# Retention stage: the first gate product among the state products, the gate products one tile ahead, the turns of finished tiles behind the outputs

## The reference, cut to what matters

```
inner = einsum('bnihd,bnjhd->bnhij', qc, kc) * dmat        # per tile of 128 tokens, 4 heads
o_inner = einsum('bnhij,bnjhe->bnihe', inner, vc)
kv = einsum('bnjhd,bnjhe->nbhde', k_dec, vc)               # per tile, forward and backward
s_end, s_start = scan(lambda s, kv_n: (chunk_decay * s + kv_n, s), s0, kv)
o_cross = einsum('bnihd,nbhde->bnihe', q_dec, s_start)
ret = head_group_norm(o_fwd + o_bwd, ret_gn) * silu(gr)    # gr: columns of the input projection
```

## Time and profile before

| | us |
|---|---|
| time, median of 3 runs (2480.75 to 2486.7) | 2484.94 |
| the profiled execution's own time | 2485.23 |
| its span, first to last instruction | 2483.4 |
| PE busy in the span (88%) | 2189.6 |
| DVE busy (48%) | 1194.3 |
| ACT busy (33%) | 811.9 |
| POOL busy (10%) | 241.3 |

### The profile page before, as it was taken

One profiled execution on the slowest core, in us unless ns is written; L12 is line 12 of the kernel. 1 busy time (PEld: TensorE's weight loads), 2 busy tenths in 40 slices (PEclk: granted clock), 3 DMA queues, 4 the chain that ended last, 5 costly groups with the idle time before them and its releaser, 6 DMA issues.

```text
span 2483.4 us, 25328 instructions
## 1 busy us (share of the span) xinstructions
PE 2189.6 (88%) x10527; PEld 1654.5 (67%) x10527; DVE 1194.3 (48%) x1490; ACT 811.9 (33%) x998; POOL 241.3 (10%) x200
## 2 busy tenths in 40 slices
PE   1999989899999969999759999997999996799992
PEld 0587765388886547777637766645888844677771
DVE  0293234232322468887556622524223235788883
ACT  1123423010000137777432244211000012577771
POOL 2132010100000020000021301002000000100002
PEclk9999989999999969999979998998999996899996
DMA  7225330211124369999641334011021133799983
GB/s 267 88 88 203 136 145 1 102 52 68 35 102 153 110 233 373 381 381 377 244 168 68 131 122 158 9 68 51 35 102 68 54 125 119 277 378 386 381 338 144
DMA packets 113877, 417.13 MB, mean 168 GB/s; under 512 B 7768, under 2 KB 9928, under 8 KB 89056
## 3 DMA queue, kind: packets, MB, share of 16 engines
q1 hardware_dynamic: 89056, 329.27, 35.7%
q0 software_dynamic: 19920, 68.31, 7.4%
q10 hardware_dynamic: 4784, 17.87, 1.8%
HBM read 378.89 MB, written 36.54 MB: 167 GB/s over the span
## 4 chain that ended last, share of the span: by engine, by line
PE 71%; DVE 16%; ACT 6%; issue 3%; DMA 3%; SPq 0%; ACTq 0%; PEldq 0%; POOL 0%; DVEq 0%; POOLq 0%
PE ps L645 60%; DVE expert_low L1827 7%; ACT expert_high L1364 2%; PE ps L760 2%; PE ps L656 2%; PE ps L773 2%; DVE x_low L1833 2%; DMA ring_lo<-in_w_mod_dram 1%; ACT branch L1397 1%; ACT x_high L1369 1%; DVE work L1852 1%; DVE hidden_low L1839 1%; DVE work L1595 1%; PE ps L911 1%; PE ps L761 1%
## 5 line engine op out<-in xcount | busy, mean ns | idle before, releaser
L1827 DVE TENSOR_TENSOR expert_low<-ring_lo,expert_high 128x2048 fp32r<-128x2048 f32 x192 | 432.9, 2285 | 26.9 <-ACT expert_high L1364 26.9
L1364 ACT ACTIVATE expert_high<-ring_lo 128x2048 fp32r<-128x2048 f32 x192 | 367.3, 1915 | 158.7 <-PE ps L645 133.1
L645 PE MATMUL ps<-ring_lo,hT 128*128 128x512 f32 (+1 forms) x800 | 314.5, 552 | 12.5 <-ACT hT L1198 12.3
L645 PEld LDWEIGHTS ps<-ring_lo,hT 128*128 128x128 f32 x800 | 150.9, 191 | 164.1 <-issue 160.4
L645 PE MATMUL ps<-expert_high,x_high 128*128 128x512 f32 x512 | 207.5, 405 | 9.6 <-DVE expert_low L1827 9.6
L645 PE MATMUL ps<-branch,ring_lo 128*128 128x320 f32 x768 | 214.4, 432 | 0.0
L645 PE MATMUL ps<-expert_high,x_low 128*128 128x512 f32 x512 | 201.9, 394 | 0.0
L645 PE MATMUL ps<-expert_low,x_high 128*128 128x512 f32 x512 | 200.9, 392 | 0.0
L1313 ACT ACTIVATE work<-ps 128x640 f32<-128x640 f32 x48 | 33.7, 703 | 501.7 <-PE ps L645 501.7
L645 PE MATMUL ps<-h_hi,w_hi 128*128 128x320 f32 x768 | 186.2, 324 | 1.7 <-issue 1.7
L645 PEld LDWEIGHTS ps<-branch,ring_lo 128*128 128x128 f32 x768 | 143.6, 190 | 53.3
(11 more groups left out here) (272 smaller groups left out, 3195.6 us busy)
## 6 DMA issues: line engine op xcount, KB each, us to landing
ring_lo<-in_w_gate_dram SPq DMA_DIRECT2D x64, 1024.0 KB, 8.4
ring_lo<-in_w_up_dram SPq DMA_DIRECT2D x64, 1024.0 KB, 7.1
ring_lo<-in_w_down_dram SPq DMA_DIRECT2D x64, 1024.0 KB, 7.5
ring_lo<-in_w_in_dram SPq DMA_DIRECT2D x26, 2048.0 KB, 7.9
ring_lo<-in_w_mod_dram SPq DMA_DIRECT2D x24, 2048.0 KB, 13.0
y_dram<-branch ACTq DMA_DIRECT2D x32, 512.0 KB, 8.9
ring_lo<-in_w_out_dram SPq DMA_DIRECT2D x4, 2048.0 KB, 8.9
work<-mod_dram POOLq DMA_DIRECT2D x12, 512.0 KB, 9.0
```

Of the source, the lines that this page charges most:

```text
L645: return pe.matmul(out, lhsT, rhs, start=(k == 0), stop=(k == n - 1))
L1364: A(e_high[n % HIGH], e_raw[n % RAW], ACT.Copy).then_inc(ec_a.sem, 1)
L1827: TT(out=e_low[n % RAW], in0=e_raw[n % RAW], in1=e_high[n % HIGH].bitcast(F32), op=ALU.subtract).then_inc(el_v.sem, 1)
```

## The change

PE makes state products 0 and 1, then the gate product of tile 0, then state products 2 to 7, then turns q and k of tile 0. In the loop it makes the gate product of the next tile, the inner product of this one, the turns of q and k of the next, the outputs of this one, and last the turn of the finished result of the tile before. Outputs now also wait until the tile before has been normed (bank 6), which the turn of that tile did earlier. Silu's result has five buffers, one for each tile, in a part of `branch` that held the zeros and the modulation rows; ACT therefore waits for the transfers out of them before the first Silu. ACT takes Silu and k one tile ahead. DVE copies q of the next tile after the outputs of this one are there, before it norms them, and waits for the turn of the tile before ahead of overwriting `o_tmp`.

```diff
--- before.py
+++ after.py
@@ -548,7 +548,7 @@
         sf_st = [w_(11776 + 512 * n, 512) for n in range(NS)]
         rqT, rqTf, rqTb, rkT = (w_(13824 + 512 * n, 512).rearrange("p (h i) -> p h i", h=HR) for n in range(4))
         inner = [w_(15872 + 512 * b, 512).rearrange("p (h i) -> p h i", h=HR) for b in range(2)]
-        sgr = w_(16896, 512)
+        sgr = [branch[:, 8 * T + 512 * t:8 * T + 512 * (t + 1)] for t in range(NT)]
         gu = w_(8192, NT * 512).rearrange("p (t c) -> p t c", t=NT)
         gv = w_(10752, NT * 512).rearrange("p (t c) -> p t c", t=NT)
         cmb = [w_(13824 + 512 * b, 512) for b in range(2)]
@@ -821,7 +821,9 @@
 
 
                 w(pe, e_a, l, NU)
-                for n, (_, tt) in enumerate(STATES):
+                def state_product(n):
+
+                    tt = STATES[n][1]
                     w(pe, kd_g, l, n + 1)
                     if n >= 2:
                         w(pe, kv_v, l, n - 1)
@@ -830,32 +832,23 @@
                         i = pe.matmul(ps[:, n % 2, hs], kdec[n % 2][:, hs], zr[:, tt, 2, hs], start=True, stop=True)
                     i.then_inc(kv_p.sem, 1)
 
-                def turn_ret(tt):
-                    w(pe, rn_v, l, tt + 1)
+                def gate_ret(tt):
+                    wt = loaded("gr")
                     if tt >= 1:
-                        w(pe, rt_ev, l, tt)
-                    for c in range(4):
-                        i = pe.transpose(ps[:, 7, c * P:(c + 1) * P], o_tmp[:, c * P:(c + 1) * P], ident)
-                    i.then_inc(rt_p.sem, 1)
-
-                w(pe, pt_a, l, NU)
-                w(pe, at_a, l, NT)
-                wt = loaded("gr")
-                w(pe, hr_g, l, 2)
-                w(pe, kv_v, l, 2 * (NS - 1))
-                w(pe, st_a, l, 2)
-                for tt in range(NT):
+                        w(pe, gr_a, l, tt)
+                    for k in range(KD):
+                        i = mm(bank(5), h3[:, k, tok(tt)], wt[:, k * 512:(k + 1) * 512], k, KD)
+                    i.then_inc(gr_p.sem, 1)
+
+                def turn_qkr(tt):
                     for src, b, sig_p, sig_e in ((0, 2, rq_p, rq_v), (1, 3, rk_p, rk_a)):
                         if tt >= 1:
                             w(pe, sig_e, l, tt)
                         for h in range(HR):
                             i = pe.transpose(ps[:, b, h * P:(h + 1) * P], zr[:, tt, src, h * P:(h + 1) * P], ident)
                         i.then_inc(sig_p.sem, 1)
-                    if tt >= 1:
-                        w(pe, gr_a, l, tt)
-                    for k in range(KD):
-                        i = mm(bank(5), h3[:, k, tok(tt)], wt[:, k * 512:(k + 1) * 512], k, KD)
-                    i.then_inc(gr_p.sem, 1)
+
+                def inner_product(tt):
                     w(pe, rq_v, l, tt + 1)
                     w(pe, rk_a, l, tt + 1)
                     if tt >= 1:
@@ -863,9 +856,11 @@
                     for h in range(HR):
                         i = pe.matmul(ps[:, 4, h * P:(h + 1) * P], rkT[:, h, :], rqT[:, h, :], start=True, stop=True)
                     i.then_inc(in_p.sem, 1)
+
+                def ret_out(tt):
+                    w(pe, in_v, l, tt + 1)
                     if tt >= 1:
-                        turn_ret(tt - 1)
-                    w(pe, in_v, l, tt + 1)
+                        w(pe, rn_v, l, tt)
                     for h in range(HR):
                         hs = slice(h * P, (h + 1) * P)
                         n = 3 if tt < NS else 1
@@ -874,6 +869,35 @@
                             mm(ps[:, 6, hs], rqTf[:, h, :], sf_st[tt][:, hs], 1, n)
                             i = mm(ps[:, 6, hs], rqTb[:, h, :], sb_st[tt][:, hs], 2, n)
                     i.then_inc(o_p.sem, 1)
+
+                def turn_ret(tt):
+                    w(pe, rn_v, l, tt + 1)
+                    if tt >= 1:
+                        w(pe, rt_ev, l, tt)
+                    for c in range(4):
+                        i = pe.transpose(ps[:, 7, c * P:(c + 1) * P], o_tmp[:, c * P:(c + 1) * P], ident)
+                    i.then_inc(rt_p.sem, 1)
+
+                state_product(0)
+                state_product(1)
+                w(pe, pt_a, l, NU)
+                w(pe, at_a, l, NT)
+                w(pe, hr_g, l, 2)
+                gate_ret(0)
+                for n in range(2, 8):
+                    state_product(n)
+                w(pe, kv_v, l, 2 * (NS - 1))
+                w(pe, st_a, l, 2)
+                turn_qkr(0)
+                for tt in range(NT):
+                    if tt + 1 < NT:
+                        gate_ret(tt + 1)
+                    inner_product(tt)
+                    if tt + 1 < NT:
+                        turn_qkr(tt + 1)
+                    ret_out(tt)
+                    if tt >= 1:
+                        turn_ret(tt - 1)
 
 
                 w(pe, kv_v, l, 8)
@@ -1284,15 +1308,24 @@
                     w(act, rt_p, l, tt + 1)
                     A(retT[:, :, tok(tt)], heads(bank(7)), ACT.Copy).then_inc(rt_ev.sem, 1)
 
-                for tt in range(NT):
+                def silu_ret(tt):
+                    w(act, gr_p, l, tt + 1)
+                    A(sgr[tt], bank(5), ACT.Silu).then_inc(gr_a.sem, 1)
+
+                def take_rk(tt):
                     w(act, rk_p, l, tt + 1)
                     if tt >= 1:
                         w(act, in_p, l, tt)
                     A(flat(rkT), bank(3), ACT.Copy).then_inc(rk_a.sem, 1)
-                    w(act, gr_p, l, tt + 1)
-                    if tt >= 1:
-                        w(act, rn_v, l, tt)
-                    A(sgr, bank(5), ACT.Silu).then_inc(gr_a.sem, 1)
+
+                act.wait_ge(y_zero, 32)
+                act.wait_ge(mod_st, 64 * NGRP * (l + 1))
+                silu_ret(0)
+                take_rk(0)
+                for tt in range(NT):
+                    if tt + 1 < NT:
+                        silu_ret(tt + 1)
+                        take_rk(tt + 1)
                     if tt >= 1:
                         take_ret(tt - 1)
                     root(l, bna[:, 0:4])
@@ -1598,16 +1631,21 @@
                     TT(out=new, in0=st_tmp, in1=bank(n % 2), op=ALU.add).then_inc(kv_v.sem, 1)
                     w(V, kv_v, l, n + 1)
                 w(V, kv_out, l, 32)
-                for tt in range(NT):
+                def take_rq(tt):
                     w(V, rq_p, l, tt + 1)
                     if tt < NS:
                         step.mark(TT(out=rqTf, in0=heads(bank(2)), in1=dec_q[:, 0], op=ALU.mult))
                         step.mark(TT(out=rqTb, in0=heads(bank(2)), in1=dec_q[:, 1], op=ALU.mult))
                     V.tensor_copy(flat(rqT), bank(2)).then_inc(rq_v.sem, 1)
+
+                take_rq(0)
+                for tt in range(NT):
                     w(V, in_p, l, tt + 1)
                     TT(out=inner[tt % 2], in0=heads(bank(4)), in1=dec_in, op=ALU.mult).then_inc(in_v.sem, 1)
 
                     w(V, o_p, l, tt + 1)
+                    if tt + 1 < NT:
+                        take_rq(tt + 1)
                     for h in range(HR):
                         step.mark(V.bn_stats(bn[:, 6 * h:6 * h + 6], bank(6)[:, h * P:(h + 1) * P]))
                     step.settle()
@@ -1616,6 +1654,8 @@
                     step.settle()
                     step.do(V.tensor_copy(bna[:, 0:4], mean_var[:, 1:8:2]))
                     inverse_root(bna[:, 0:4], bna[:, 4:8], 1.0)
+                    if tt >= 1:
+                        w(V, rt_p, l, tt)
                     for h in range(HR):
                         hs = slice(h * P, (h + 1) * P)
                         step.mark(TS(out=o_tmp[:, hs], in0=bank(6)[:, hs], scalar1=mean_var[:, 2 * h:2 * h + 1],
@@ -1623,7 +1663,7 @@
                     step.settle()
                     step.do(TT(out=o_tmp, in0=o_tmp, in1=ret_gain, op=ALU.mult))
                     w(V, gr_a, l, tt + 1)
-                    TT(out=o_tmp, in0=o_tmp, in1=sgr, op=ALU.mult).then_inc(rn_v.sem, 1)
+                    TT(out=o_tmp, in0=o_tmp, in1=sgr[tt], op=ALU.mult).then_inc(rn_v.sem, 1)
 
                 V.tensor_copy(h_hi, hT[:, :]).then_inc(hh_v.sem, 1)
 
```

## The result

The changed kernel takes 2488.88 us (median of 16 executions, 2487.51 to 2492.15), the kernel before 2484.55 in the same series (2480.75 to 2486.85): a ratio of 1.0016, 95% interval 1.0009 to 1.0024, which is 4.3 us slower and within 0.3%. The profiled execution took 2487.78 us, its span is 2486.0.

A forecast was written before the change was run, and what follows sets the result against it. PE was taken to bound the tiles and a Vector engine chain the states. States +11.8, tiles -8.4 and clock falls +3.8 sum to +7.2 us on the 2484.94 median: 2492.1 us, range 2487.0 to 2495.0.

The forecast's parts named there:

- states: First state product to first turn: gate block lengthens it 4.9 and 5.8 us, slow clock adds 0.6 and 0.45; +11.8.
- tiles: Tile loop up to the mu products: covered waits and the moved gate product make it 4.2 us shorter a layer.
- clock behind the hole: Last tile: clock falls to half level in both layers, slowing outputs and mu product, 1.9 us each; +3.8 us.
- stage in all: Retention stage, both layers: +3.4 us without clock falls, plus 3.8 for the falls, +7.2 us.
- Rival (b): Early gate block among the states runs at half clock throughout, together +19.9 us, 2504.8; chance 0.06.
- (d): Gate block among the states waits for its weights, so the move does nothing; chance 0.05, near no change.
- The last tile: Tile 4: masking stands behind tile 3's norm, so PE idles about 4.8 us before the last outputs.
- rival (c): Last tile does not wait: outputs 4.05 us earlier a layer, no clock fall, -4.7 us, 2480.2; chance 0.07.
- upper bound of 2.3: Most a clock fall behind the last tile's hole could cost, in us: half level for 4.6 us.
- Rival (a): Last tile's hole costs its length, but the clock falls in one layer or none: 2490.2 or 2488.3; chance 0.32.
- the price of the row: Table load before the square root in tile 3's norm: about 1.28 us by the trace, without the skill's drain.

The follow-up runs named there:

- e0: The changed kernel itself, timed once more beside the other runs: 2487.21 us, ratio 1.0009 to the kernel before.
- e9: Changed kernel with each gate product back in its own tile, keeping the new order of turns and copies and five Silu buffers: 2483.91 us, ratio 1.0002.
- e2: Changed kernel with the first mu product moved into the last tile's hole, ahead of its outputs: 2474.05 us, ratio 0.9956 to the kernel before.
- e7: Changed kernel with the last tile's masking put ahead of tile 3's norm on the Vector engine: 2492.16 us, ratio 1.0030 to the kernel before.
- e8: Changed kernel, last tile's masking ahead of tile 3's norm, its outputs in bank 5, turns of tiles 3 and 4 behind mu products: 2479.30 us, ratio 0.9979.
- e1: Changed kernel with ten products that nothing reads put in the last tile's hole: 2495.09 us, ratio 1.0043 to the kernel before.
- e1b: Changed kernel with five products that nothing reads put in the last tile's hole: 2486.81 us, ratio 1.0011 to the kernel before.
- e5: Changed kernel with the first gate product cut into eight slices spread ahead of state products 2 to 6: 2483.04 us, ratio 0.9992 to the kernel before.
- e4: Kernel before with only tile 0's gate product moved among the state products, loop order kept: 2491.97 us, ratio 1.0037 to the kernel before.

## Why the prediction was nearly right

The forecast was 2492.1, a change of +7.2 us, and the range 2487.0 to 2495.0; 2488.88 lies in it, 3.2 us below the forecast, a change of +4.3. The steps, one by one:

| term, both layers, us | forecast | first profile | e0 |
|---|---|---|---|
| states | +11.8 | +9.3 | +11.4 |
| tiles | -8.4 | -9.2 | -9.1 |
| clock behind the hole | +3.8 | +4.0 | +5.2 |
| stage in all | +7.2 | +4.1 | +7.4 |

(The clock's part is what outputs, turn and mu product took on the chain of waits beyond 1.0, 0.44 and 6.87 us: 1.8 and 2.2 us in the first profile, 2.7 and 2.5 in e0. The tiles are the rest of the stage; terms are rounded.)

**States.** The mechanism held: two products, the block, and then the Vector engine's chain as before, 9.67 us from 350.23 to 359.90 against 9.9. The size was off: this is the term that was mis-sized, by 2.5 us in the first profile and 0.4 in e0, and the stretch to the first turn is 19.3 and 19.9 us, then 20.8 and 20.4, where 20 to 21 were named. The prediction took 3.5 us for the first two products and 1.05 us for a slow block; in the first profile the clock rose at about 342.5, in the middle of the products (0.85 in the row 342 to 344), which took 2.68 us, and the block ran its 6.87 at full level. In e0 it rose later and the block was slow. Rival (b), half level throughout, did not happen, and neither did (d): the block starts at 343.52 right behind the second state product, without a wait for its weights.

**Tiles and turns.** The tile's wait was covered, gate products came 11.92 us apart (11.5 to 11.9 forecast), and e9 finds the gain of this part by itself in the stage: 4.4 us in both layers.

**The last tile.** The hole of 4.37 us was forecast at about 4.8, released by the masking with the norm before it, as said. e2 shows that it is the loss. One sentence of rival (c) was wrong, that only the Vector engine's order speaks against it: e7 removes that order and is no faster, since the outputs also wait for bank 6, by a wait that the diff adds and the change's description names. With both gone e8 is 4.7 us faster than before; the rival was priced at -4.7. That the two agree so closely is partly luck: e8 also moves two turns, and its stages are 6.2 us shorter than before.

**The clock.** It fell in both layers, in both profiles of the changed kernel; e1 and e1b keep PE busy there and have no fall. The size is partly luck. The 3.9 us at half level came from the hole that ends at 498.72; behind the nearest hole, the one of 4.1 us, the kernel before stays at half level to 878, with work for PE in every row, which the prediction did not read:

```profile
876.00:878.00 2.00, 2.00 (x16) 0.50 0.17 12
```

A fall cost 1.8 to 2.7 us, and in e0 both lie above the prediction's upper bound of 2.3. Rival (a), one fall or none, gives nearly the measured medians, but not by its mechanism.

**Silu and the table.** The root of tile 3 starts at 410.14, right behind the 1.28 us load at 408.85; the price of the row held, and the 2.66 us that the Trainium skill gives (ScalarE: Activation LUTs, "What ACT_TABLE_LOAD costs") was not seen here.

What stays open is the step from stage to median. The stages of two executions say +4.1 and +7.4, the whole profiled times +2.6 and +5.8 (2487.78 and 2491.07 against 2485.23), the medians +4.3 and +3.5. In these two executions the code behind layer 1's stage took 2.0 and 0.9 us less than in the profile before; why was not followed up. The clock's falls outside the stage differ between other profiles by some 3 us (below), but which of them the other executions had was not seen. e0's stage has the forecast's +7.2 almost to the microsecond, the first profile's little more than half of it; the measured +4.3 lies between +2.6 and +5.8, and the range took in all of them.

## What to carry to other kernels

When a product moves one iteration ahead, look at the last iteration: it has lost the work that covered its waits, and here that gave back more than the covered waits of the other tiles had saved. Put the next stage's first product there (e2), and feed a chain of another engine in pieces near the size of its holes (here of 0.9 and 1.7 us) rather than in one block (e5); together they turned 4 us of loss into 17 of gain. Before an order is blamed for a wait, list all waits of the late instruction, the buffer it writes among them: e7 took away one of two and gained nothing. And ask of each wait whether its signal comes when the buffer is free, or later.

## What was not expected of the hardware

The clock also falls without a long wait: in e4 PE was busy 1.13 and 1.16 us in the two rows ahead of the fall and never idle for more than 1.70 us at a time, and two products more made the tile shorter. And unchanged code takes two different times: the stretch shown under e9 lasts 28.5 us in nine of the fourteen profiles and 31.7 in five (e1, e1b, e4c, e7, e9), with no time between. Its mean granted clock is 0.64 or 0.65 in the five and 0.69 to 0.74 in the nine. What decides between the two was not tested; that shifts of a few microseconds ahead of the stretch do it is a guess. About 3 us can be lost or gained far from the edit, and gains of that size in a stage (e1b, e9) need not show in the time.
